# Copying turned tiles with two engines, turning the convolution rows into four quarters, and starting the down samples before the last up copies

## The reference

```
h = RMSNorm(x)
rq, rk, rv, rg, aq, ak, av, gr, ga = split(h @ w_in)
branch A: retention with q and k rotated, chunks of 128, 4 heads, a state per head
branch B: dilated window attention, 3 groups x 4 heads, against cached keys and values for the samples
mix = sigmoid(gr) * (A @ w_branch_ret) + sigmoid(ga) * (B @ w_branch_attn)
x = x + RMSNorm(mix @ w_out)
u = RMSNorm(x) @ w_ffn_up                     # 5632 columns
c = conv_b + sum(conv_w[i] * ext[:, i:i+T] for i in range(3))
f = (gelu(c[:, :2816]) * c[:, 2816:]) @ w_ffn_down
x = x + RMSNorm(f)
```

## Time and profile before

| | us |
|---|---|
| median of three runs | 1027.38 |
| lowest and highest of them | 1025.37, 1028.23 |
| the profiled execution, its own time | 1025.77 |
| its span, from first to last instruction | 1023.9 |
| TensorE busy | 988.2 (97%) |
| VectorE busy | 548.9 (54%) |
| ScalarE busy | 384.6 (38%) |
| GpSimd busy | 188.2 (18%) |
| mean granted clock of TensorE | 0.995 of full |

### The profile page before, as it was taken

One profiled execution on the slowest core, in us unless ns is written; L12 is line 12 of the kernel. 1 busy time (PEld: TensorE's weight loads), 2 busy tenths in 40 slices (PEclk: granted clock), 3 DMA queues, 4 the chain that ended last, 5 costly groups with the idle time before them and its releaser, 6 DMA issues.

```text
span 1023.9 us, 20316 instructions
## 1 busy us (share of the span) xinstructions
PE 988.2 (97%) x7730; PEld 879.5 (86%) x7730; DVE 548.9 (54%) x894; ACT 384.6 (38%) x848; POOL 188.2 (18%) x379
## 2 busy tenths in 40 slices
PE   5999999999999999999999889999999999999997
PEld 4777777778999899999887679999999999777775
DVE  5354125425376887783155576666666666422226
ACT  6233232441543333333133744444444444212413
POOL 2102004134162344445110001000000001011000
PEclk9999999999999999999999999999999999999999
DMA  6734544545696576769634324554544553222323
GB/s 238 264 133 152 178 159 167 185 152 177 258 305 221 194 239 195 235 200 324 196 114 141 123 76 162 171 169 170 188 164 173 174 192 115 85 89 68 105 83 116
DMA packets 40914, 175.36 MB, mean 171 GB/s; under 512 B 7259, under 2 KB 7707, under 8 KB 39313
## 3 DMA queue, kind: packets, MB, share of 16 engines
q1 hardware_dynamic: 25616, 125.78, 35.6%
q0 software_dynamic: 15232, 48.65, 14.9%
HBM read 164.40 MB, written 54.05 MB: 213 GB/s over the span
## 4 chain that ended last, share of the span: by engine, by line
PE 85%; DVE 5%; ACT 3%; DMA 3%; issue 2%; SPq 0%; POOL 0%; DVEq 0%; ACTq 0%
PE bank L1338 10%; PE bank L1340 10%; PE bank L1339 9%; PE bank L1844 9%; PE bank L1845 8%; PE bank L1846 8%; PE bank L1418 5%; PE bank L1422 5%; PE bank L1421 5%; PE bank L1357 3%; DMA wraw<-in_weights 2%; ACT whi L818 1%; DMA qbc<-sample_queries 1%; PE bank L1751 1%; PE bank L1320 1%
## 5 line engine op out<-in xcount | busy, mean ns | idle before, releaser
L1921 DVE TENSOR_TENSOR wlo<-wraw,whi 128x1024 fp32r<-128x1024 f32 x89 | 108.7, 1223 | 289.0 <-ACT whi L818 288.9
L818 ACT ACTIVATE whi<-wraw 128x1024 fp32r<-128x1024 f32 x91 | 96.4, 1059 | 351.4 <-PE bank L1340 236.3
L1844 PE MATMUL bank<-T1h,whi 128*128 128x288 f32 (+1 forms) x704 | 202.5, 288 | 3.1 <-DVE T1l L1931 1.7
L1845 PE MATMUL bank<-T1l,whi 128*128 128x288 f32 (+1 forms) x704 | 203.6, 289 | 0.0
L1846 PE MATMUL bank<-T1h,wlo 128*128 128x288 f32 (+1 forms) x704 | 203.2, 289 | 0.0
L1844 PEld LDWEIGHTS bank<-T1h,whi 128*128 128x128 f32 x704 | 133.0, 189 | 3.8 <-issue 1.9
L1845 PEld LDWEIGHTS bank<-T1l,whi 128*128 128x128 f32 x704 | 132.7, 189 | 0.0
L1846 PEld LDWEIGHTS bank<-T1h,wlo 128*128 128x128 f32 x704 | 132.3, 188 | 0.0
L1338 PE MATMUL bank<-whi,T1h 128*128 128x512 f32 (+1 forms) x288 | 113.9, 396 | 0.8 <-DVE wlo L1921 0.3
L1418 PE MATMUL bank<-T1h,whi 128*128 128x272 f32 x384 | 113.4, 295 | 0.0
L1422 PE MATMUL bank<-T1h,wlo 128*128 128x272 f32 x384 | 111.0, 289 | 0.0
(11 more groups left out here) (302 smaller groups left out, 1832.7 us busy)
## 6 DMA issues: line engine op xcount, KB each, us to landing
wraw<-in_weights SPq DMA_DIRECT2D x142, 512.0 KB, 3.7
out_s_kv_g<-in_cache_kv_g SPq DMA_DIRECT2D x64, 511.0 KB
qbc<-sample_queries POOLq DMA_DIRECT2D x48, 256.0 KB, 4.8
kvk<-in_cache_kv_g POOLq DMA_DIRECT2D x32, 256.0 KB, 4.2
kvv<-in_cache_kv_g POOLq DMA_DIRECT2D x16, 512.0 KB, 7.9
out_s_kv_g<-in_cache_kv_g SPq DMA_DIRECT2D x16, 508.0 KB
S<-in_state_ret POOLq DMA_DIRECT2D x16, 256.0 KB, 3.2
out_s_ret<-S POOLq DMA_DIRECT2D x16, 256.0 KB, 6.0
```

Of the source, the lines that this page charges most:

```text
L818: nc.scalar.activation(w_halves(s)[0], wraw[:, s % 2, :], ACT.Copy).then_inc(w_hi, 1)
L1844: mm(dst, Wh, T1h[:, k, c], start=k == 0, stop=False)
L1845: mm(dst, Wh, T1l[:, k, c], start=False, stop=False)
L1921: v.tensor_tensor(lo, wraw[:, s % 2, :], hi.bitcast(F), ALU.subtract).then_inc(w_lo, 1)
```

## The change

It has three parts.

1. **Turned tiles copied by two engines.** ScalarE copies tiles 0 and 2 ahead of its weight split and tile 4 behind it; VectorE copies tiles 1 and 3 ahead of its own weight split. The banks of retention are exchanged: O in 7 and 5 instead of 6 and 7, U in 6 instead of 5, Os in 7 instead of 6, the first two Us in 5 and 6 instead of 7 and 5.
2. **Convolution rows in four quarters.** The 44 tiles are turned by plain products with the unit matrix, four a step, each into 18 rows of another quarter of the partitions (0, 32, 64, 96); quarter q takes tiles 11q to 11q + 10. Three banks hold all of it, VectorE copies three times (128 rows, after steps 3, 7 and 10), and GpSimd issues eight stores at the end. The wait for the last tail goes to the first of these steps.
3. **The first down samples.** The wait for the last copies of the up stage (`columns_read`) goes behind the sample products of down slots 0 and 1.

```diff
@@ psum_uses
-        order += [(("O", c, 0), 6), (("O", c, 1), 7), (("U", c, 0), 5), (("U", c, 1), 5)]
-        order += [(("Os", c), 6)] + [(("Us", c, p), (7, 5)[p]) for p in range(2)]
+        order += [(("O", c, 0), 7), (("O", c, 1), 5), (("U", c, 0), 6), (("U", c, 1), 6)]
+        order += [(("Os", c), 7)] + [(("Us", c, p), (5, 6)[p]) for p in range(2)]
...
-    order += [(("cv", j), 5 + j % 3) for j in range(2 * FT // 4)]
+    order += [(("cv", j), 5 + j) for j in range(3)]
@@ buffers
-    cvrow = sb("cv_row", U0 + 1024, [128, 2, 512])
+    cvrow = sb("cv_row", U0 + 1024, [128, FT // 2 * 128])
@@ both engines
+    def turned_views(bi, b, i):
+        n = rows(i)
+        src = b[:, 0:4 * n].rearrange("p (k n) -> p k n", k=4)
+        for dst, d0, s0, k in turned_parts(bi):
+            to, of = dst[:, d0:d0 + k, cols(i)], src[:, s0:s0 + k, :]
+            if dst is aqT and i < 4:
+                to = to.rearrange("p k (r j) -> p k r j", r=4)
+                of = of.rearrange("p k (j r) -> p k r j", r=4)
+            yield to, of
@@ gpsimd
-        for j in range(2 * FT // 4):
+        for j in range(3):
             emptied(pool, ("cv", j))
-            pool.dma_start(o["p_conv"][0, 0, :, 512 * j:512 * j + 512], cvrow[0:2, j % 2, :]).then_inc(cv_out[j % 2], 16)
-            pool.dma_start(o["s_conv"][0].rearrange("b t n -> (b t) n")[:, 512 * j:512 * j + 512], cvrow[2:18, j % 2, :]
-                           ).then_inc(cv_out[j % 2], 16)
+        for q in range(4):
+            c = slice(FT // 2 * 128 * q, FT // 2 * 128 * (q + 1))
+            pool.dma_start(o["p_conv"][0, 0, :, c], cvrow[32 * q:32 * q + 2, :]).then_inc(cv_out, 16)
+            pool.dma_start(o["s_conv"][0].rearrange("b t n -> (b t) n")[:, c], cvrow[32 * q + 2:32 * q + 18, :]).then_inc(cv_out, 16)
@@ scalar, the projection's loop
+                turned = s == 1 and bi in (1, 2, 5, 6, 7)
+                if turned:
+                    turn_evac(bi - 1, 0)
+                    turn_evac(bi - 1, 2)
                 w_split(first + s + 2)
-                if s == 1 and bi in (1, 2):
-                    turn_evac(bi - 1)
-                if s == 1 and bi in (5, 6, 7):
-                    turn_evac(bi - 1)
+                if turned:
+                    turn_evac(bi - 1, 4)
@@ tensor
+                if s == 0 and opening:
+                    opening()
                 last_two = tail == 2 and s == n - 1
...
-        pe.wait_ge(u_evac[0], FT + 1)
-        pe.wait_ge(u_evac[1], FT + 1)
-        pe.wait_ge(tail_done, 2 * FT + 4)
+        def columns_read():
+            pe.wait_ge(u_evac[0], FT + 1)
+            pe.wait_ge(u_evac[1], FT + 1)
...
         def conv_tail(s):
-            if s < 11:
+            if s == 0:
+                pe.wait_ge(tail_done, 2 * FT + 4)
+            if s < FT // 2:
                 turn18(s)
...
-        def turn18(j):
-            b, full = open_bank(("cv", j))
-            for k in range(4):
-                last = nc.tensor.transpose(b[0:18, 128 * k:128 * k + 128], cvt[:, 18 * (4 * j + k):18 * (4 * j + k) + 18], ident)
-            last.then_inc(full, 1)
+        def turn18(s):
+            key, at_ = ("cv", s // 4), 128 * (s % 4)
+            b = P[USES[key][0]]
+            if s % 4 == 0:
+                open_bank(key)
+            for q in range(4):
+                tile = FT // 2 * q + s
+                last = mm(b[32 * q:32 * q + 18, at_:at_ + 128], cvt[:, 18 * tile:18 * tile + 18], ident, start=True, stop=True)
+            if s % 4 == 3 or s == FT // 2 - 1:
+                last.then_inc(bank_full[USES[key][0]], 1)
@@ vector
+        def turn_evac(bi, i):
+            b = filled(dve, ("t", bi, i))
+            for to, of in turned_views(bi, b, i):
+                ins = v.tensor_copy(to, of)
+            ins.then_inc(bank_free[USES[("t", bi, i)][0]], 1)
...
+                if s == 1 and bi in (1, 2, 5, 6, 7):
+                    turn_evac(bi - 1, 1)
+                    turn_evac(bi - 1, 3)
                 w_split(first + s + 2)
...
-            if j >= 2:
-                dve.wait_ge(cv_out[j % 2], 32 * (j // 2))
-            v.tensor_copy(cvrow[0:18, j % 2, :], b[0:18, :]).then_inc(bank_free[USES[key][0]], 1)
+            at_ = 512 * j
+            w = min(512, FT // 2 * 128 - at_)
+            v.tensor_copy(cvrow[:, at_:at_ + w], b[:, 0:w]).then_inc(bank_free[USES[key][0]], 1)
...
-            if s < 11:
-                conv_rows(s)
+            if s in (3, 7, 10):
+                conv_rows(s // 4)
```

More of the change, by code:

```diff
@@ L393, in build_layer @@
     fjunk = sb("fjunk", U0, [128, D])
[L394 to L395 removed]
+    cvrow = sb("cv_row", U0 + 1024, [128, FT // 2 * 128])
+    assert U0 + 1024 + FT // 2 * 128 <= U0 + 6 * UW
     def cav(name, *shape):
@@ L464, in build_layer @@
     y_out = sem("y_out")
-    cv_out = [sem(f"cv_out{n}") for n in range(2)]
+    cv_out = sem("cv_out")
     def emptied(eng, key):
@@ L484, in w_halves, with turned_parts @@
         return whi[:, s % 2, :], wlo[:, s % 2, :]
+    def turned_parts(bi):
+        return {BLK_RQ: ((qT, 0, 0, 4),), BLK_RK: ((kT, 0, 0, 4),), BLK_AQ: ((aqT, 0, 0, 4),),
+                BLK_AQK: ((aqT, 4, 0, 2), (akT, 0, 2, 2)), BLK_AK: ((akT, 2, 0, 4),)}[bi]
+    def turned_views(bi, b, i):
[7 more added lines that the diff above has]
+            yield to, of
     def by_class(t):
@@ L793, in _ @@
         pool.wait_ge(av_out, 16 * (NG + 1))
-        for n in range(2):
-            pool.wait_ge(cv_out[n], 32 * (6 - n))
+        pool.wait_ge(cv_out, 16 * 8)
     @block.scalar
@@ L860, in evac_block @@
                 ins.then_inc(b_free[i], 1)
[L862 to L882, removed]
-                    ins = nc.scalar.activation(to, of, ACT.Copy)
-                ins.then_inc(bank_free[USES[("t", bi, i)][0]], 1)
+        def turn_evac(bi, i):
+            b = filled(act, ("t", bi, i))
+            for to, of in turned_views(bi, b, i):
+                ins = nc.scalar.activation(to, of, ACT.Copy)
+            ins.then_inc(bank_free[USES[("t", bi, i)][0]], 1)
         def half_squares(first_bi, x, junk_, base):
@@ L1321, in turn, with b_block @@
             last.then_inc(full, 1)
-        def b_block(bi, Th, Tl, Ts, between=None, ready=None, operand=None, tail=1, ahead=0):
+        def b_block(bi, Th, Tl, Ts, between=None, ready=None, operand=None, opening=None, tail=1, ahead=0):
             first, n, per, w = BLOCKS[bi]
@@ L1892, in conv_tail @@
         def conv_tail(s):
-            if s < 11:
+            if s == 0:
+                pe.wait_ge(tail_done, 2 * FT + 4)
+            if s < FT // 2:
                 turn18(s)
-        def turn18(j):
-            b, full = open_bank(("cv", j))
-            for k in range(4):
-                last = nc.tensor.transpose(b[0:18, 128 * k:128 * k + 128], cvt[:, 18 * (4 * j + k):18 * (4 * j + k) + 18], ident)
-            last.then_inc(full, 1)
+        def turn18(s):
[8 more added lines that the diff above has]
+                last.then_inc(bank_full[USES[key][0]], 1)
         b_block(BLK_DN, lambda k, c: fh[:, k, c], lambda k, c: fl[:, k, c], lambda k: fs[:, k, :], between=conv_tail,
-                operand=lambda k: pe.wait_ge(f_lo, k + 2))
+                operand=lambda k: pe.wait_ge(f_lo, k + 2), opening=columns_read)
         b_block(BLK_DN + 1, lambda k, c: fh[:, k, c], lambda k, c: fl[:, k, c], lambda k: fs[:, k, :], tail=2)
@@ L2054, in sample_outputs, with turn_evac @@
                     step(ins)
-            ins.then_inc(bank_free[6], 1)
+            ins.then_inc(bank_free[USES[("Os", h)][0]], 1)
+        def turn_evac(bi, i):
+            b = filled(dve, ("t", bi, i))
+            for to, of in turned_views(bi, b, i):
+                ins = v.tensor_copy(to, of)
+            ins.then_inc(bank_free[USES[("t", bi, i)][0]], 1)
         for bi in range(BLK_OUT):
```

## The result

The changed kernel takes **1019.91 us** (median of 5 executions, 1018.28 to 1021.04) against 1027.38 (5 executions, 1025.27 to 1028.23): a ratio of 0.9924, interval 0.9905 to 0.9944. Its profiled execution took 1019.37 us, with a span of 1017.6 at a granted clock of 0.994; the one of before had 1025.77, 1023.9 and 0.995.

The account below looks back on a forecast made before the run. TensorE was taken as the bound nearly everywhere, with 85% of the chain that ended last. The terms -3.8 + 2.2 - 1.4 - 0.7 = -3.7 us, from 1026.7, gave 1023.0; range 1020.3 to 1026.8.

Parts of the forecast that it names:

- Blocks 5 and 7: Turning in blocks 5 and 7: two copying engines and exchanged banks let `outputs` start 1.1 us earlier in each.
- Block 6: Turning in block 6, where ScalarE came to the copies still later: `outputs` at 208.5 instead of 210.13, 1.6 us less.
- Block 2: Turning in block 2: VectorE's copy of tile 1 delays tile 4 and the sample products, 0.8 us lost.
- Block 1: Turning in block 1: VectorE's copy of tile 1, between its two weight splits, delays tile 4's load, 1.4 us lost.
- the first ends near 59.4: Block 1: the first of VectorE's two weight splits, run back to back from 58.20, ends then, before its tile copy.
- The opening: First down sample products moved ahead of the wait for the last up-stage copies: 1.4 us less, range 1.0 to 1.5.
- The convolution rows: First down half, quarter products for turnings: six steps gain 0.22, five lose 0.11; 0.7 us gained.
- (c): Convolution rows: an 18-column operand does not run beside its neighbours, 6.4 us lost, 1030.1; chance 0.08.
- (d): Blocks 5 to 7: VectorE is behind there too, so the 3.8 gain falls to about nothing, 1026.8; chance 0.09.
- (b): Sample-key chain between 300 and 470, paced by transfers, takes back the turning blocks' net 1.6: 1024.6; chance 0.15.
- (a): Convolution rows: change of shape is free, quarter products cost 0.22 every step; 1.7 us more gained, 1021.3; chance 0.08.
- the four together have a mean of 1026.7: Starting time of the forecast: mean of the profiled execution, 1025.77, and the three runs with median 1027.38.

Follow-up runs that it names:

- before_a: The kernel before, unchanged, run once more for another trace; the kernel before has a median of 1027.38 us.
- before_c: The kernel before, unchanged, run once more for its trace; the kernel before has a median of 1027.38 us.
- best12_odd: Changed kernel, but in blocks 1 and 2 VectorE copies only tile 3, ScalarE the rest; convolution turnings only at steps where samples follow: 1017.12 us, ratio 0.9909.
- wait6: Changed kernel with eight small ScalarE copies ahead of its first copy in block 6: median 1022.36 us, ratio 0.9963.

## Why the prediction was wrong, point by point

**Blocks 5 and 7: right in mechanism, slightly under-sized.** Forecast 1.1 each, measured 1.28. The term that was too large was the 0.2 for a change of shape between tile 4's turnings, 32 rows deep, and `outputs`: from 171.55, where tile 4's weight loads begin, to `outputs` at 171.92 there are 0.37, of which the loads are 0.32. Only 0.05 is left.

**Block 6: the same.** Forecast 1.6, measured 1.81. Together 4.36 against 3.8, just beyond the better bound of 4.3, in which strided copies were free. They are (0.69 against 0.67), so the bound at 0.3 a block needn't have been taken into the middle.

**Block 2: right.** Forecast 0.8 lost, measured 0.79, with VectorE's copy as releaser.

**Block 1: right in mechanism, sized from a scattered number.** Forecast 1.4 lost, measured 0.78. The step that failed is "the first ends near 59.4": it took the start of VectorE's two splits, 58.20, for a property of the program. They started 58.20 - 56.26 = 1.94 after the first turning, which in the trace of the record is

```profile
56.26 1.47 PE L1320 MATMUL bank<-ca,rope_q 128*128 128x128 f32 x12
```

In `before_a`, the same code, VectorE's and TensorE's timelines have

```profile
57.38 2.34 DVE L1921 TENSOR_TENSOR wlo<-wraw,whi 128x1024 fp32r<-128x1024 f32 x2
```

```profile
56.00 1.47 PE L1320 MATMUL bank<-ca,rope_q 128*128 128x128 f32 x12
```

and so 1.38, and in all the other traces 1.37 or 1.38. In the execution of the record one of the first weight slots had landed later than in `before_c`, whose first turning starts at the same time (56.30). ScalarE's split of that slot, in the record and in `before_c`:

```profile
41.16 1.06 ACT L818 ACTIVATE whi<-wraw 128x1024 fp32r<-128x1024 f32 x1 [8.31 <-DMA wraw<-in_weights]
```

```profile
39.48 1.06 ACT L818 ACTIVATE whi<-wraw 128x1024 fp32r<-128x1024 f32 x1 [6.49 <-DMA wraw<-in_weights]
```

Of these 1.7 us VectorE was still 0.6 late in block 1. Block 2, one block later, had lost that lateness, and its forecast of 0.8 would have been the right one for block 1 too: the code is the same and the two sat side by side in my sum with different prices.

**The opening: right.** Forecast 1.4 (1.0 to 1.5), measured 1.49: the first down product comes 1.27 behind the last up product, where I had put 875.1 - 873.78 = 1.32.

**The convolution rows: right, a little more.** Forecast 0.7, measured 0.97. A lonely step was costed at 0.55 for its eight instructions; with 877.70 - 876.69 = 1.01, less two pitches of 0.23, it takes 0.55. A step with samples behind it, forecast 0.22, takes 942.52 - 942.29 = 0.23:

```profile
941.97 0.39 PE L1341 MATMUL bank<-whi,fTl 128*128 128x512 f32 x1
942.29 0.41 PE L1909 MATMUL bank<-ca,cv_tail 128*18 128x128 f32 x8
942.52 1.06 PE L1358 MATMUL bank<-wraw,fTs 128*32 128x128 f32 x32
943.50 0.50 PE L1339 MATMUL bank<-whi,fTh 128*128 128x512 f32 x1
```

The forecast of 6 x 0.22 - 5 x 0.11 is 0.77 before rounding. A pair of steps, from one group of sample products to the next, takes 896.52 - 883.38 = 13.14 instead of 13.29, so 0.15 less where 0.11 was forecast; over five pairs that is the other 0.2. The stores in a bunch took what was forecast (eight issues from 946.29 to 950.29) and nobody waited for them.

**The rivals.** (c), that 18 columns would not run beside each other, is refuted: eight instructions in 0.23. (d) is refuted by 2.30, 2.36, 2.30. (b), that the early savings are taken back between 300 and 470, is refuted too: from block 7's outputs to the first sample-key scores TensorE takes 89.59 before and 89.61 after, and from there, through the stretch in question, to the first product of the output projection 202.09 and 201.98. That second length scatters by some 0.7 between traces without a fall of the clock in it (201.4 to 202.1), which is less than the 1.6 at stake. Of (a), half is right: the quarter products do cost 0.22, but the change of shape is not free, as 1.55 us in `best12_odd` show. The Trainium skill, page TensorEngine Tiling (Array Packing), section Tiling Modes, says that a change of mode drains the engine. The runs agree, at 0.33 for both changes around a step. The factor of up to 4 that the Trainium skill gives in the Overview of that page does not come out here: a lonely step got slower, 0.55 for the 0.44 of four turnings, and one beside other quarter work twice as fast.

**What no step had: the clock.** The term that I left out is the 1.6 us (0.5) timed beyond the starts; 1.0 to 1.1 of it is clock that the old kernel loses and the new one mostly doesn't, by the mean granted clocks, and only about 0.5 has a place, behind block 6. I counted from "the four together have a mean of 1026.7", which was right, but I took a gain on TensorE's line to be a gain of the same size in time: the sum has no term for the clock, which behind the long pause of block 6 falls in some executions. The record's trace could not have shown it, since its clock behind block 6 is 1.00; its mean of 0.995 against 0.9934 over 82 executions only says that it was a luckier one. Without this term the time would have been 1026.7 - 5.25 = 1021.5, inside the range: the sum of the steps was 1.5 too small, and what put the time outside is this.

**The sum.** -3.7 became -6.8 in the mean: 0.6 from block 1, 0.6 from blocks 5 to 7, 0.1 from the opening, 0.2 from the rows, 1.6 from what no step had, mostly clock. The first four end at most 0.25 beyond the better bound of their term (the farthest: 1.57 lost in blocks 1 and 2 together, where the bound was 1.8); all five errors had the same sign. The range ended at 1020.3, the bound of rival (a) with the better turnings. With block 1 costed as block 2 and free strided copies the same steps give 1026.7 - 4.9 = 1021.8.

## What to carry to other kernels

Before a single trace's gap between two engines is used as a price, look whether the same code has another gap one repetition later; here the difference, early in the program, was the arrival of one weight slot, and the later gap was the price. Where several engines empty what TensorE writes, look first at which bank the next product asks for: here that alone was half the gain of blocks 5 to 7, and giving the late engine the bank that is asked for last turned a loss of 0.8 into a gain of 0.6 a block. Put small work in quarters next to other work in quarters, where it costs its instructions only.

## What the runs showed of the hardware that I had not expected

**A wait can cost more than its length, behind its end, and only in some executions.** TensorE ran at a granted clock of 1.00, 2.4 GHz, up to block 6 and through its turnings, 4.17 us with two waits of 0.81 and 0.90 in them, and in two traces of seven the clock stood at 0.57 from 210 to 214 us, that is mostly at the lower level of 1.2 GHz, for 1.7 us lost. With 5.12 us of it the one trace has 0.53 over 6 us and 2.95 lost (its clock falls just before the last wait ends, 0.90 from 205 to 211), and 12 executions have a mean 2 us above what the starts account for. None of the nine traces with 3.9 or less in block 6 has it; one of them has 4.05 in blocks 5 and 7. The Trainium skill, page TensorE: Matmul & The Clock Gate, Part 1, says that the gate follows the recent activity of the engine and judges it at moments that don't follow the kernel's start, so that the same kernel is met by it or not; that the same code showed both agrees, but `wait6`, with 4.23 and no fall in its one trace, shows that a single trace can't tell. Whether the two waits bring it, or the whole stretch with its turnings, no run here separates.

**Quarter products of 18 columns start some 0.03 us apart**, as those of 32 do: eight in 0.23, sixteen in 0.45, where four turnings of the same width took 0.44.

**A copy out of PSUM in a strided order costs VectorE hardly anything extra**: 0.69 against 0.67 for 512 elements, and ScalarE 0.60 either way.
